# Sample-first order of a first stage on one Trainium2 core, with output-weight splitting moved off GpSimd

## What is computed

```python
xn = rms_norm(x, norm1_w)
hq, hf_f, hf_b, hi, hg, aq, ak, av = jnp.split(xn @ w_in, split_points(), axis=-1)
o_hg = hgrn2_bidirectional(hq, hf_f, hf_b, hi, hg, lb_f, lb_b, hg_norm_w)
o_da = diff_attention(aq, ak, av, layer, q_norm_w, k_norm_w, lq1, lk1, lq2, lk2, subln_w)
h = x + jnp.concatenate([o_hg, o_da], axis=-1) @ w_out
return h + expert_choice_moe(rms_norm(h, norm2_w), router_w, w1, w3, w2)
```

## Time and profile before

| | |
|---|---|
| time, median of 3 runs | 2092.39 us (2090.39 to 2092.54) |
| profiled execution, its own time | 2092.09 us |
| its span, first to last instruction | 2090.3 us |
| PE busy | 2015.9 us, 96% of the span |
| DVE, ACT, GpSimd busy | 1618.4, 1335.0, 118.0 us |
| DMA | 618.15 MB, mean 296 GB/s |

### The profile page before, as it was taken

The page is one execution under the profiler, slowest core; times in us unless marked ns, Lnnn a source line. Parts: engine busy times, 40 slices in busy tenths (PEclk is TensorE's granted clock), DMA queues, the critical chain, the costliest instruction groups (busy, mean ns, idle before and its releaser), DMA issues.

```text
span 2090.3 us, 27776 instructions
## 1 busy us (share of the span) xinstructions
PE 2015.9 (96%) x10730; PEld 1547.7 (74%) x10730; DVE 1618.4 (77%) x1186; ACT 1335.0 (64%) x1021; POOL 118.0 (6%) x62
## 2 busy tenths in 40 slices
PE   6999999979499999999999999999999999999998
PEld 5899998757467777777777777777777777777776
DVE  4247766763778888888888888888888888888886
ACT  4234433632277777777777777777777777777774
POOL 0000000330200000000000000000000000000000
PEclk9999999989799999999999999999999999999999
DMA  4222224125399999999999999999999999999994
GB/s 152 75 64 78 94 76 166 64 68 207 126 343 366 388 355 397 359 387 368 381 379 371 389 358 393 358 389 373 380 377 364 395 360 395 357 387 365 387 383 153
DMA packets 192387, 618.15 MB, mean 296 GB/s; under 512 B 13680, under 2 KB 38000, under 8 KB 192336
## 3 DMA queue, kind: packets, MB, share of 16 engines
q1 hardware_dynamic: 188640, 604.86, 77.1%
q0 software_dynamic: 3696, 12.59, 2.6%
HBM read 596.96 MB, written 20.45 MB: 295 GB/s over the span
## 4 chain that ended last, share of the span: by engine, by line
PE 92%; DVE 4%; DMA 2%; ACT 1%; issue 1%; SPq 0%; POOL 0%; POOLq 0%; ACTq 0%; DVEq 0%
PE pair L573 28%; PE pair L575 28%; PE pair L574 28%; PE pair L634 2%; PE pair L903 1%; DMA hg<-projected 1%; PE pair L707 1%; PE pair L731 1%; DVE mixed L1562 1%; PE pair L851 1%; PE pair L692 1%; PE pair L718 0%; DMA x_in<-x 0%; PE pair L674 0%; DVE mix_low L1497 0%
## 5 line engine op out<-in xcount | busy, mean ns | idle before, releaser
L1681 DVE TENSOR_TENSOR chunk_low<-ring,chunk_high 128x2048 fp32r<-128x2048 f32 (+1 forms) x382 | 1175.5, 3087 | 224.5 <-ACT chunk_high L1156 224.5
L1156 ACT ACTIVATE chunk_high<-ring 128x3072 fp32r<-128x3072 f32 (+1 forms) x384 | 981.2, 2564 | 212.6 <-PE pair L575 212.3
L573 PE MATMUL pair<-chunk_high,xe_high 128*96 128x512 f32 (+1 forms) x1536 | 579.3, 377 | 1.3 <-DVE xe_low L1675 1.3
L575 PE MATMUL pair<-chunk_high,xe_low 128*96 128x512 f32 (+1 forms) x1536 | 575.0, 374 | 0.0
L574 PE MATMUL pair<-chunk_low,xe_high 128*96 128x512 f32 (+1 forms) x1536 | 573.2, 373 | 0.0
L573 PEld LDWEIGHTS pair<-chunk_high,xe_high 128*96 128x96 f32 x1536 | 248.2, 162 | 90.2 <-DVE chunk_low L1681 2.7
L575 PEld LDWEIGHTS pair<-chunk_high,xe_low 128*96 128x96 f32 x1536 | 247.8, 161 | 90.1
L574 PEld LDWEIGHTS pair<-chunk_low,xe_high 128*96 128x96 f32 x1536 | 248.5, 162 | 87.3
L573 PE MATMUL pair<-chunk_high,hid_high 128*96 128x512 f32 x704 | 280.3, 398 | 0.0
L575 PE MATMUL pair<-chunk_high,hid_low 128*96 128x512 f32 x704 | 276.9, 393 | 0.0
L574 PE MATMUL pair<-chunk_low,hid_high 128*96 128x512 f32 x704 | 276.2, 392 | 0.0
(11 more groups left out here) (207 smaller groups left out, 1875.1 us busy)
## 6 DMA issues: line engine op xcount, KB each, us to landing
ring<-w SPq DMA_DIRECT2D x288, 1536.0 KB, 9.3
ring<-w SPq DMA_DIRECT2D x96, 1024.0 KB, 8.3
raw_w<-w_in SPq DMA_DIRECT2D x16, 1024.0 KB, 5.6
projected<-stage SPq DMA_DIRECT2D x36, 128.0 KB, 1.7
wo_raw<-w_out SPq DMA_DIRECT2D x8, 512.0 KB, 3.4
x_in<-x SPq DMA_DIRECT2D x6, 512.0 KB, 7.9
queries_and_keys<-qk_raw SPq DMA_DIRECT2D x8, 384.0 KB, 2.6
x_again<-x SPq DMA_DIRECT2D x6, 512.0 KB, 4.7
```

The lines of the kernel that those rows point to most:

```text
L573: pe.matmul(dst, a_high, b_high, start=first, stop=False)
L575: return pe.matmul(dst, a_low, b_high, start=False, stop=last)
L1156: act.activation(ch[c % SPLIT][:, 0:n], ring[c % RING][:, 0:n], ACT.Copy).then_inc(ch_done, 1)
L1681: dve.tensor_tensor(cl[c % SPLIT][:, 0:n], ring[c % RING][:, 0:n], ch[c % SPLIT][:, 0:n].bitcast(F32), ALU.subtract).then_inc(cl_done, 1)
```

## The change

First stage: piece 0 of `w_in` is loaded behind the fourth x tile, piece 1 as soon as piece 0 is split. The statistics and scaling of the two prompt tiles move behind the split of the sample tiles and of piece 0. PE transposes four tiles, runs the sample columns of unit 0, then transposes the prompt tiles, then the sample columns of unit 1 and the prompt columns of both. The head norm weights load later.

Attention: ACT makes the high halves of output weights 5 to 7 (units 18, 20, 22), DVE their low halves (5 at 19; 6 and 7 behind `mix_low(0)`), and ACT the attention squares of tiles 3 to 5. SP loads `hg` three tiles ahead and ahead of the chunk.

Routing: six sample rounds ahead of the last `residual`; `moe_rows` of the last tile ahead of the last rounds; chunk 1's low half on DVE behind the first rows' split, so GpSimd makes one low half; the ring loads 5, 6, 7 in this order.

```diff
@@ -69,9 +69,10 @@
 WO_AT = 10
-WO_BOTH_AT = {16: 5, 19: 6, 20: 7}
+WO_LATE_AT = {18: 5, 20: 6, 22: 7}
 NORM_AT = 20
 MIX_AT = 24
+WO_LOW_AT = 19
 PROBS = 3
@@ -83,7 +84,7 @@
 SAMPLE_ROUNDS = CAP_S // 8
-ROUNDS_DURING = 5
+ROUNDS_DURING = 6
 SLOTS = CAP_P + CAP_S
@@ -257,6 +258,7 @@
     masks_in = sem("masks_in")
+    head_norms_in = sem("head_norms_in")
     masks_done = sem("masks_done")
@@ -372,7 +374,7 @@
-    NCONST = 7
+    NCONST = 5
@@ -457,9 +459,8 @@
                     sp.dma_start(norm1_bc[:, :], norm1.partition_broadcast(P)).then_inc(norm1_in, 16)
-            load_piece(sp, 0)
-            for i, w in enumerate((hgw, subw)):
-                sp.dma_start(norm_w[:, i:i + 1], w.rearrange("(p o) -> p o", o=1)).then_inc(consts_in, 16)
+                if i == SAMPLE_TILES - 1:
+                    load_piece(sp, 0)
             for i, w in enumerate((qw, kw)):
@@ -469,11 +470,15 @@
+            sp.wait_ge(wl_done, 1)
+            load_piece(sp, 1)
             sp.wait_ge(x_t, TILES)
...
-
-            for hc in range(FM_PIECES + 1):
+            for i, w in enumerate((hgw, subw)):
+                sp.dma_start(norm_w[:, i:i + 1], w.rearrange("(p o) -> p o", o=1)).then_inc(head_norms_in, 16)
+
+
+            for hc in range(1, FM_PIECES + 1):
                 sp.wait_ge(wl_done, hc + 1)
@@ -533,12 +538,16 @@
                 sp.dma_start(norm2_t[:, :], norm2.rearrange("(k p) -> p k", p=P)).then_inc(norm2_in, 16)
+            def load_hg(t):
+                sp.wait_ge(mix_rdy, t - 1)
+                sp.dma_start(hg[t % 2][:, :], tm_d[tile(ORDER[t]), HW:2 * HW]).then_inc(hg_in[t % 2], 16)
+
+            load_hg(2)
             for t in range(TILES):
+                if t + 3 < TILES:
+                    load_hg(t + 3)
                 if t >= 1:
                     load_chunk(sp, 0, t - 1)
-                if t + 2 < TILES:
-                    sp.wait_ge(mix_rdy, t + 1)
-                    sp.dma_start(hg[t % 2][:, :], tm_d[tile(ORDER[t + 2]), HW:2 * HW]).then_inc(hg_in[t % 2], 16)
@@ -550,12 +559,11 @@
+            sp.wait_ge(xe_in, 16)
+            load_chunk(sp, 0, RING - 1)
             sp.wait_ge(early_low, 1)
...
-
-            sp.wait_ge(xe_in, 16)
-            load_chunk(sp, 0, RING - 1)
-            sp.wait_ge(early_low, 2)
+            sp.wait_ge(cl_done, EARLY)
             load_chunk(sp, 0, RING + 1)
@@ -576,32 +584,46 @@
         pe.wait_ge(ident_in, 16)
-        for i, t in enumerate(ORDER):
+        def transpose_x(i):
             pe.wait_ge(xs_ready, i + 1)
...
             for k in range(KT):
-                mm = pe.transpose(pair[2 + i % 2][:, tile(k)], x_scaled[:, t, tile(k)], ident[:, :])
+                mm = pe.transpose(pair[2 + i % 2][:, tile(k)], x_scaled[:, ORDER[i], tile(k)], ident[:, :])
             mm.then_inc(x_t, 1)
-        for u in range(FM_UNITS):
+        def feature_major(u, part):
             hc = u // 2
-            if u % 2 == 0:
-                pe.wait_ge(wl_done, hc + 1)
-            if u >= 2:
-                if u - 2 < HEADS:
-                    pe.wait_ge(q_done, u - 1)
-                else:
-                    pe.wait_ge(fm_act, u - 1)
-            dst = pair[u % 2]
+            d0, d1, x0, x1, tiles = ((0, SAMPLE, PROMPT, T, SAMPLE_TILES), (512, 512 + PROMPT, 0, PROMPT, TILES))[part]
             cols = slice((u % 2) * P, (u % 2 + 1) * P)
-            for d0, d1, x0, x1, tiles in ((0, SAMPLE, PROMPT, T, SAMPLE_TILES), (512, 512 + PROMPT, 0, PROMPT, TILES)):
-                if u == 0:
-                    pe.wait_ge(xl_done, tiles)
-                for k in range(KT):
-                    mm = split_mm(dst[:, d0:d1], wh[hc % 2][:, k, cols], wl[hc % 2][:, k, cols],
-                                  xh[:, k, x0:x1], xlo[:, k, x0:x1], k == 0, k == KT - 1)
-            mm.then_inc(fm_mm, 1)
+            if part == 0:
+                if u % 2 == 0:
+                    pe.wait_ge(wl_done, hc + 1)
+                if u >= 2:
+                    if u - 2 < HEADS:
+                        pe.wait_ge(q_done, u - 1)
+                    else:
+                        pe.wait_ge(fm_act, u - 1)
+            if u == 0:
+                pe.wait_ge(xl_done, tiles)
+            for k in range(KT):
+                mm = split_mm(pair[u % 2][:, d0:d1], wh[hc % 2][:, k, cols], wl[hc % 2][:, k, cols],
+                              xh[:, k, x0:x1], xlo[:, k, x0:x1], k == 0, k == KT - 1)
+            if part == 1:
+                mm.then_inc(fm_mm, 1)
+
+        for i in range(SAMPLE_TILES):
+            transpose_x(i)
+        for u in range(2):
+            feature_major(u, 0)
+            if u == 0:
+                transpose_x(SAMPLE_TILES)
+                transpose_x(SAMPLE_TILES + 1)
+        for u in range(2):
+            feature_major(u, 1)
+        for u in range(2, FM_UNITS):
+            for part in range(2):
+                feature_major(u, part)
@@ -938,15 +960,20 @@
         act.activation(rstd1[:, :], rstd1[:, :], ACT.Sqrt)
-        for g in range(3):
+        for g in range(2):
             squares(2 * g)
...
         high_part(0)
-        for i in range(2, TILES):
-            x_high(i)
+        x_high(2)
+        x_high(3)
+        squares(4)
+        squares(5)
+        std(2)
+        x_high(4)
+        x_high(5)
         high_part(1)
@@ -1038,6 +1065,11 @@
+        def attention_squares(i):
+            act.wait_ge(o_red, i)
+            act.wait_ge(ao_ev, i + 1)
+            act.activation(sq_o[:, 512:1024], mixed[:, i, 512:1024], ACT.Square).then_inc(o_sq, 1)
+
@@ -1073,6 +1105,8 @@
                 evac_attention(done)
+                if done >= SAMPLE_TILES - 1:
+                    attention_squares(done)
             if a < ATT_UNITS:
@@ -1083,6 +1117,9 @@
                 w_out_high(a - WO_AT)
+            if a in WO_LATE_AT:
+                act.wait_ge(go_mm, TILES)
+                w_out_high(WO_LATE_AT[a])
             if a == MIX_AT + 1:
@@ -1233,14 +1270,14 @@
         scale(3)
+        x_low(0)
+        x_low(1)
+        low_part(0)
+        x_low(2)
+        x_low(3)
         mean_and_rstd(2)
         scale(4)
-        x_low(0)
         scale(5)
-        x_low(1)
-        x_low(2)
-        x_low(3)
-        low_part(0)
         x_low(4)
@@ -1262,8 +1299,7 @@
         dve.reciprocal(lb_max[:, :, :], lb_max[:, :, :]).then_inc(setup_v, 1)
-        dve.tensor_scalar(qk_w[:, 0, :], qk_w[:, 0, :], QK_DIM ** -0.5, None, ALU.mult)
-        dve.tensor_scalar(norm_w[:, 1:2], norm_w[:, 1:2], 1.0 - LAM_INIT, None, ALU.mult).then_inc(setup_v, 1)
+        dve.tensor_scalar(qk_w[:, 0, :], qk_w[:, 0, :], QK_DIM ** -0.5, None, ALU.mult).then_inc(setup_v, 1)
         dve.wait_ge(setup_v, 10)
@@ -1409,6 +1445,8 @@
+        dve.wait_ge(head_norms_in, 32)
+        dve.tensor_scalar(norm_w[:, 1:2], norm_w[:, 1:2], 1.0 - LAM_INIT, None, ALU.mult)
         dve.wait_ge(masks_in, 16)
@@ -1497,6 +1535,10 @@
+
+        def w_out_low(k):
+            dve.wait_ge(woh_done, k + 1)
+            dve.tensor_tensor(wol[k][:, :], wo_raw[k % 2][:, :], woh[k][:, :].bitcast(F32), ALU.subtract).then_inc(wol_done, 1)
@@ -1524,8 +1566,12 @@
                 mix(1)
+            if a == WO_LOW_AT:
+                w_out_low(WO_EARLY)
             if a == MIX_AT + 1:
                 mix_low(0)
+                w_out_low(WO_EARLY + 1)
+                w_out_low(WO_EARLY + 2)
         attention_reduce(TILES - 1)
@@ -1639,6 +1685,7 @@
         h_reciprocal(t)
+        moe_rows(t)
         top_tokens(0, ROUNDS_DURING)
@@ -1647,8 +1694,6 @@
             top_round(1, r)
-            if r == 0:
-                moe_rows(t)
         for r in range(ROUNDS_DURING + 2, SAMPLE_ROUNDS):
@@ -1701,12 +1746,13 @@
-        dve.wait_ge(early_low, EARLY)
-        dve.sem_inc(cl_done, EARLY)
+        dve.wait_ge(early_low, 1)
+        dve.sem_inc(cl_done, 1)
         dve.wait_ge(route_done, 4)
...
         rows_low(1, 2)
+        chunk_low(0, 1)
         with dve.Fori(0, EXPERTS - 1) as e:
@@ -1732,11 +1778,6 @@
-        def w_out_high(k):
-            pool.wait_ge(go_mm, TILES)
-            pool.wait_ge(wo_in[k % 2], 16 * (k // 2 + 1))
-            pool.tensor_copy(woh[k][:, :], wo_raw[k % 2][:, :]).then_inc(woh_done, 1)
-
@@ -1746,17 +1787,13 @@
                 w_out_low(a - WO_AT)
-            if a >= HEADS + 3 and (a - 3) % HEADS == 0:
+            if a >= HEADS + 3 and (a - 3) % HEADS == 0 and (a - 3) // HEADS < SAMPLE_TILES:
                 attention_squares((a - 3) // HEADS - 1)
-            if a in WO_BOTH_AT:
-                w_out_high(WO_BOTH_AT[a])
-                w_out_low(WO_BOTH_AT[a])
-
-
-        for c in range(EARLY):
-            n = chunk_size(c)
-            pool.wait_ge(ch_done, c + 1)
-            pool.tensor_tensor(cl[c][:, 0:n], ring[c][:, 0:n], ch[c][:, 0:n].bitcast(F32), ALU.subtract).then_inc(early_low, 1)
+
+
+        n = chunk_size(0)
+        pool.wait_ge(ch_done, 1)
```

(1 more changed line is left out.)

## The result

The changed kernel takes 2077.55 us (median of four runs, 2075.94 to 2080.89) against 2092.2 (four runs, 2090.39 to 2092.54): ratio 0.9934, 95% interval 0.9917 to 0.9951. The same kernel measured again gave 2076.06 (ratio 0.9924, 0.9907 to 0.9940). The second trace of that kernel has a span of 2087.7 and the repeat of the changed one 2075.4, so by the traces the gain is 12.3 to 15.6.

A forecast was written before the change was run, and what follows sets the result against it. PE was taken to bound the experts' stage, its start set by the chain before it. The terms -0.9 + 2.7 + 3.7 + 6.8 = 12.3 us earlier took 2092.09 to 2079.8 us, range 2075.8 to 2084.8.

The forecast's parts named there:

- First stage: Start to unit 2: unit 0 starts 4.5 us earlier, less 3.5 for prompt transposes, less 1.9 for clock: 0.9 later.
- The step that failed: First stage: the prompt tiles' transposes between the sample columns of units 0 and 1 cost PE 3.5 us.
- The second step: First stage: unit 0 starts at the low clock, nine matmuls at the slow pace, 1.9 us lost.
- End of attention: Before the output projection: DVE steps stretched beside GpSimd's weight splitting go, so `mix_low(0)` ends 2.7 us earlier.
- (d): End of attention: ACT becomes the bound and 2.5 of the 2.7 us are lost: 2082.3; chance 0.10.
- Projection: Output projection: earlier `hg` and ACT's squares end most waits for `mix_low` and the residual: gain 3.7 us.
- Routing: Before the experts: unstretched `moe_rows` and a moved round; the cast still waits for GpSimd; PE's transposes start 6.8 us earlier.
- (b): Experts' stage: paced by DMA, so the chunk now loaded during routing costs 4.2 us again: 2084.0; chance 0.10.
- (c): Output projection: `hg` still lands late behind other transfers and the 3.7 us stay: 2083.5; chance 0.08.
- (e): First stage: PE stays at low clock, losing 0.47 per us; 12.3 gone after 26 us, 2095.3 with 33; chance 0.03.

The follow-up runs named there:

- second trace of that kernel: The kernel before the change, unaltered, traced once more: one run, 2089.5 us.
- PE kept busy: The changed kernel plus 27 identity transposes that nobody reads on PE before unit 0: 2076.53 us, ratio 0.9930.
- the kernel of both parts: The changed kernel plus idle transposes in three places, DVE making chunk 0's low half, and a semaphore increment behind the first gather: 2075.96 us, ratio 0.9921.

## Why the prediction was right

The sign, the mechanism of three of the four parts and the sum held. The sum was 12.3 against 15.6 of the span; the terms:

**First stage: forecast 0.9 later, measured 0.4 earlier.** The start of unit 0 was right (4.5 forecast, 27.65 - 22.82 = 4.8). The step that failed is the price of the prompt tiles' transposes. I took 3.5 for 16, from the 3.52 of the first two tiles, which I read as full clock. Behind unit 0 they took 32.73 - 31.06 = 1.67. Both of my rows were at the slow pace of 0.22 a transpose; one at the fast pace was in the same trace, not among my rows: eight transposes of a mix in 1.03 at 458.76. The second step was low in this trace: nine matmuls at the slow pace for 1.9 were forecast and 13 came, (28.50 - 22.82) - 3.06 = 2.6, the 3.06 being the same 13 with PE kept busy. 4.8 - 1.7 - 2.6 = 0.5 against the 0.4 that is seen. The errors offset each other in part, +1.8 and -0.7. The count is not fixed: of the eight traces with the new order and no busy transposes four have 7 slow matmuls and four 12 or 13, so the 1.9 lies between. Over these eight traces unit 2 starts at 42.5 to 44.6, against 44.4 to 44.7 with the old one; the stage alone is worth nothing that a measurement tells.

**End of attention: 2.7 forecast, 3.8 between the two traces, 2.1 to 3.0 at like clock.** The stalls went as forecast, and the root came at 431.39 (432.0 forecast). The trace of before had the last steps at the low clock (its transposes of the mix took 1.91 at 443.01), that of the changed kernel at the high one, and in the same program it falls either way: 34.7 in seven traces with the new split, 32.9 in three. Low against low is 36.78 - 34.71 = 2.1 or 37.64 - 34.71 = 2.9, high against high 35.97 - 32.98 = 3.0; 2.7 lies between. The sum of stretches that it rests on, 3.5, was made from a 2.64 that no other trace has; the others have as much in more and shorter pieces. Another 0.8 came ahead of unit 16; the second trace of the kernel before has it too (62.95), so it is scatter. Rival (d) falls: ACT's copies stand in the timeline, but `mix_low(0)` is 3.8 earlier counted from unit 16 (442.81 for 447.81 on the clock of the span, of which 1.2 came before), where (d) leaves 0.2. PE's waits for ACT's `probs_t` are 9.9 in five places for 8.7 in four; no root, copy or square of ACT stands as a releaser of PE.

**Projection: 3.7 forecast, 4.05 measured to PE's last matmul, 3.4 of it in the waits.** The waits for `mix_low` fell from 2.1 to 0.3, those for the residual ahead of the last tile's from 2.1 to 0.5: 1.8 + 1.6. Putting the load back costs 3.4 to PE's last matmul, and putting the output weights and squares back 0.24 (88.98 for 88.74). The remaining 0.4 I can't place; the two traces of the kernel before differ by 0.2. The sixth round made the last residual late by 0.7, as forecast (the wait of 2.0, for 1.3).

**Routing: 6.8 forecast, 6.66 measured**, from the end of PE's work in the projection to the first expert matmul, between two traces in both of which the router's matmuls ran slow (3.13 and 3.42). Undoing it brings back 6.0 with them at 2.55, 6.8 at like clock; against the second trace of the kernel before, with 1.93, it is 5.6. The forecast chain held step by step: `moe_rows` at 1.28 for 1.2, the write landed in time but for 0.4, the cast released by GpSimd.

**Luck in the sum.** 12.3 against 14.7 in the medians, and 12.3 to 15.6 in the traces, is close for another reason than four right terms: the first stage was 1.3 off and the clock at the end of attention and in the routing moves those terms by about 1 us from trace to trace.

**Rivals.** (b), (c) and (d) fall as told. (e), slower: the clock did stay low, but for 5.7 us of unit 0 and not for 26. Its price of 0.47 for each us holds (2.6 for 5.7 is 0.46).

## What to carry to other kernels

Before work is moved, ask at which clock the row ran from which it is priced: the same kind of 16 transposes took 3.65 or 1.91 us. Starting PE earlier by making it idle more often can cost as much as it brings (4.8 earlier, 4.4 given back); idle transposes in three such places together brought 4 us, in the first place alone nothing that the median shows. A load behind a large one in a queue shows as a long wait, and two engines that block each other as a stretched instruction of a short kind; the first gave back 3.4 us of the projection, the second 5.4 us of one `moe_rows` (6.70 to 1.28).

## What the runs showed that I had not expected

**The slowness of GpSimd's gather beside DVE.** The block seen at the cast also works the other way: an indirect DMA's issue took 4.24 instead of 1.16, 3.08 more, beside a DVE subtraction of 3.36 with two SBUF inputs that had started 0.15 earlier. The issue ended 1.03 after the subtraction had (557.28 and 556.25).

The Trainium skill (SBUF — State Buffer, "Who interferes with whom") says that such an operation takes only the read interface of the shared pair, against GpSimd instructions that read SBUF, and that writing descriptors needs the write one, which it marks as inferred. By the inference the gather would have stayed at 1.16; the traces differ and decide. By the rule for reads it would wait if its token list in SBUF is read over that interface; I can't tell which access waited.

The experts' stage shows the same with nothing changed for it. In the changed kernel the gathers for experts 2 to 15 are issued while a subtraction of DVE runs that began 0.9 to 1.7 earlier; they take 2.56 to 3.37, and each ends some 0.87 after that subtraction. The one at 559.81, begun 0.21 before the next subtraction, takes 0.99. DVE and GpSimd:

```profile
667.52 3.36 DVE L1726 TENSOR_TENSOR chunk_low<-ring,chunk_high 128x3072 fp32r<-128x3072 f32 x1 [0.41 <-ACT chunk_high L1193]
...
559.81 0.99 POOL L1764 DMA_INDIRECT xe<-moe_rows,token  x1 [5.59 <-PE pair L873]
...
668.84 2.91 POOL L1764 DMA_INDIRECT xe<-moe_rows,token  x1 [8.65 <-DMA y<-y_rows,token]
```

**A semaphore increment passes the gather.** Placed behind an indirect DMA on GpSimd it did not hold DVE until the issue had ended (550.75 against 550.91 + 4.24), nor in the kernel of both parts (549.28 against 549.43 + 4.24).

**The clock record at the start.** At 10 to 14 us the windows show 1.00, yet 16 transposes took 3.65, the pace of the low level; later, at 1.00, they took 1.91. In the repeat it goes on into unit 0: a window at 1.00, in which the matmuls are 0.43 apart.

```profile
24.00:26.00 2.00, 2.00 (x6) 1.60 (x5) 1.81 (x3) 0.13 (x1) 0.00 (x0) 1.00 0.43 153
...
24.01 0.63 PE L583 MATMUL pair<-x_high,w_low 128*128 128x512 f32 x1
```

There the granted clock alone can't be trusted, and the durations tell the level. The prediction's 3.5 for the prompt transposes came from such a window.

**Scatter by clock.** One program differs by 1 to 1.7 us in a stage from trace to trace, as the level falls around a short idle time. A term of that size is to be read between traces at like clock; the median of a few runs doesn't settle it.
